# Router bookkeeping of a mixture-of-experts step on one core: float32 against bf16 operands for the counting and list products

## The reference

```python
g_logits = (x @ rgw + rgb).astype(jnp.float32)
g_sel = jnp.argmax(g_logits, axis=-1)
e_logits = (x @ rew + reb).astype(jnp.float32).reshape(-1, N_GROUPS, EXPERTS_PER_GROUP)
e_sel = jnp.take_along_axis(e_logits, g_sel[:, None, None], axis=1)[:, 0]
top_v, top_i = lax.top_k(e_sel, TOP_K_IN_GROUP)
...
for e in range(N_EXPERTS):
    h = jax.nn.silu(x @ wg[e]) * (x @ wu[e])
    y = y + gates[:, e:e + 1] * (h @ wd[e]).astype(jnp.float32)
```

## Time and profile before

| what | value |
|---|---|
| median of 3 runs | 1059.52 us (1059.48, 1059.52, 1064.51) |
| profiled execution | 1065.51 us, of which 1063.3 us is the span |
| PE busy | 935.1 us, 88% of the span |
| DVE, ACT, POOL busy | 380.2, 238.3, 81.6 us |
| mean granted TensorE clock | 0.936 |
| memory traffic | 208.76 MB, 196 GB/s on average |

### The profile page before, as it was taken

The page is one execution under the profiler, slowest core; times in us unless marked ns, Lnnn a source line. Parts: engine busy times, 40 slices in busy tenths (PEclk is TensorE's granted clock), DMA queues, the critical chain, the costliest instruction groups (busy, mean ns, idle before and its releaser), DMA issues.

```text
span 1063.3 us, 15679 instructions
## 1 busy us (share of the span) xinstructions
PE 935.1 (88%) x6393; PEld 495.7 (47%) x6393; DVE 380.2 (36%) x806; ACT 238.3 (22%) x600; POOL 81.6 (8%) x96
## 2 busy tenths in 40 slices
PE   3996999999999999978978997899998978892996
PEld 3453556654547676665435554443333423341442
DVE  3205645562325747354542125221111111112345
ACT  3116212220123223353212112110000000001335
POOL 1000000000004533000000000100000000002100
PEclk9999999997999989978688999899999989997998
DMA  6454233033246662164603606379999999995101
GB/s 208 178 218 178 31 139 139 4 137 142 79 167 221 235 192 82 42 216 139 198 10 114 259 22 256 127 275 347 378 394 401 402 396 388 407 405 208 41 22 61
DMA packets 72099, 208.76 MB, mean 196 GB/s; under 512 B 15937, under 2 KB 48148, under 8 KB 67548
## 3 DMA queue, kind: packets, MB, share of 16 engines
q1 hardware_dynamic: 57344, 184.73, 46.9%
q0 software_dynamic: 3936, 14.22, 4.0%
q10 hardware_dynamic: 10748, 8.80, 2.6%
HBM read 188.31 MB, written 38.25 MB: 213 GB/s over the span
## 4 chain that ended last, share of the span: by engine, by line
PE 71%; DMA 11%; DVE 10%; ACT 4%; issue 2%; SPq 1%; ACTq 0%; POOL 0%; DVEq 0%; POOLq 0%
PE ps L1930 17%; DMA EXPERT<-in_moe_w_up 9%; PE ps L2354 8%; PE ps L1935 8%; PE ps L2240 6%; PE ps L2460 6%; PE ps L2389 3%; PE ps L2363 3%; PE ps L1965 2%; PE ps L2309 2%; PE ps L2011 1%; PE ps L2092 1%; PE ps L2038 1%; PE ps L1939 1%; PE ps L1914 1%
## 5 line engine op out<-in xcount | busy, mean ns | idle before, releaser
L1930 PE MATMUL ps<-xT,EXPERT 128*128 128x512 f32 x384 | 182.1, 619 | 1.2 <-DVE EXPERT L1263 1.2
L2354 PE MATMUL ps<-EXPERT,aF 128*32 128x512 f32 x1024 | 117.3, 611 | 20.5 <-DMA EXPERT<-in_moe_w_up 12.2
L1935 PE MATMUL ps<-EXPERT,xT 128*128 128x384 f32 (+1 forms) x384 | 121.7, 459 | 1.6 <-ACT EXPERT L917 1.6
L1930 PEld LDWEIGHTS ps<-xT,EXPERT 128*128 128x128 f32 x384 | 71.4, 196 | 79.5 <-issue 75.8
L1935 PEld LDWEIGHTS ps<-EXPERT,xT 128*128 128x128 f32 x384 | 78.8, 238 | 24.6 <-issue 3.5
L2354 PEld LDWEIGHTS ps<-EXPERT,aF 128*32 128x32 f32 x1024 | 34.3, 112 | 99.4 <-issue 81.2
L2460 PE MATMUL ps<-EXPERT 128*128 128x512 f32 x128 | 58.7, 618 | 5.3 <-DVE EXPERT L1891 5.3
L2389 PE MATMUL ps<-EXPERT,dF 128*32 128x512 f32 x512 | 58.2, 595 | 3.3 <-ACT dF L1168 3.3
L2240 PE MATMUL ps<-EXPERT,xT 128*128 128x512 f32 x128 | 60.0, 621 | 1.1 <-ACT xT L1087 1.1
L1843 DVE TENSOR_TENSOR dF<-dF,ps 64x512 f32<-64x512 f32 x16 | 11.0, 690 | 138.6 <-ACT dF L1164 138.6
L1164 ACT ACTIVATE dF<-ps 64x512 f32<-64x512 f32 x16 | 9.4, 590 | 207.4 <-PE ps L2354 207.4
(11 more groups left out here) (439 smaller groups left out, 1234.8 us busy)
## 6 DMA issues: line engine op xcount, KB each, us to landing
EXPERT<-in_moe_w_gate SPq DMA_DIRECT2D x16, 2048.0 KB, 15.9
EXPERT<-in_moe_w_up SPq DMA_DIRECT2D x16, 2048.0 KB, 20.9
EXPERT<-in_moe_w_down SPq DMA_DIRECT2D x16, 2048.0 KB, 21.8
EXPERT<-in_w_in SPq DMA_DIRECT2D x13, 1536.0 KB, 6.6
out_win_sample<-in_cache_win SPq DMA_DIRECT2D x16, 1022.0 KB
aF<-in_cache_k_diff SPq DMA_DIRECT2D x32, 192.0 KB, 2.5
aF<-in_cache_v_diff SPq DMA_DIRECT2D x32, 192.0 KB, 2.5
Yd<-wk ACTq DMA_DIRECT2D x34, 128.0 KB, 9.0
```

The source lines that it names most:

```text
L1930: last = t.matmul(ps[:, u % 2, :], W_[:, c, c0:c0 + w], xT[:, c, 0:SEQ], start=(c == 0), stop=(c == DC - 1))
L1935: last = t.matmul(ps[:, u % 2, 0:w], rows_, W_[:, c, c0:c0 + w], start=(c == 0), stop=(c == DC - 1))
L2354: last = t.matmul(ps[32 * q:32 * q + 32, 2, :], xgT[:, c, 32 * (q % 2):32 * (q % 2) + 32], w[:, c, :], start=(c == 0), stop=(c == DC - 1))
```

## The change

C, the ones, tri, Rsel and Tsel become bf16. Zeros, ones and counts of at most two are exact in bf16; a token number up to 519 is not. So the number is split in two exact parts, the low seven bits and the rest (a multiple of 128), and Tsel has twice as many columns of data: for each block 33 with the low part and 33 with the high part. The sums stay float32 in PSUM. The list step thus has 20 products in place of ten. POOL sets a bf16 table of ones; DVE makes the parts once, ahead of the first residual addition.

```diff
+        parts = take(2 * T5, 2)
-        C = take(T5, NE)
+        C = take(T5 * NE // 2, dt=BF16).rearrange("p (i e) -> p i e", i=T5)
-        Tsel = take(2 * T5, MAXT)
+        hot = take(T5 * MAXT, dt=BF16).rearrange("p (m j) -> p m j", m=2 * T5)
+        Tsel = take(2 * T5 * MAXT, dt=BF16).rearrange("p (m a j) -> p m a j", m=2 * T5, a=2)
-        Rsel = dF_[:, 0:2 * T5 * P].rearrange("p (m n) -> p m n", m=2 * T5)
+        Rsel = dF_[:, 0:T5 * P].bitcast(BF16).rearrange("p (m n) -> p m n", m=2 * T5)
...
             seq(g.memset(tri, 1.0))
+            seq(g.memset(onesb, 1.0))
...
             seq(v.tensor_tensor(tokf, tokf, valid, ALU.mult))
+            seq(v.tensor_copy(iti[:, 0:T5], tokf))
+            seq(v.tensor_scalar(iti[:, T5:2 * T5], iti[:, 0:T5], P - 1, None, ALU.bitwise_and))
+            seq(v.tensor_tensor(iti[:, 0:T5], iti[:, 0:T5], iti[:, T5:2 * T5], ALU.subtract))
+            for k in range(2):
+                v.tensor_copy(parts[:, k * T5:(k + 1) * T5, 0], iti[:, T5:2 * T5])
+                seq(v.tensor_copy(parts[:, k * T5:(k + 1) * T5, 1], iti[:, 0:T5]))
...
-            seq(v.tensor_tensor(Tsel, iotaf[:, 0:MAXT].unsqueeze(1).to_broadcast([P, 2 * T5, MAXT]), f2(tk, MAXT), ALU.is_equal))
-            v.tensor_tensor(Tsel.rearrange("p (k i) j -> p k i j", k=2), Tsel.rearrange("p (k i) j -> p k i j", k=2),
-                            tokf.unsqueeze(1).unsqueeze(3).to_broadcast([P, 2, T5, MAXT]), ALU.mult).then_inc(S_["rank_ok"], 1)
+            seq(v.tensor_tensor(hot, iotaf[:, 0:MAXT].unsqueeze(1).to_broadcast([P, 2 * T5, MAXT]), f2(tk, MAXT), ALU.is_equal))
+            v.tensor_tensor(Tsel, hot.unsqueeze(2).to_broadcast([P, 2 * T5, 2, MAXT]), f3(parts, MAXT),
+                            ALU.mult).then_inc(S_["rank_ok"], 1)
...
-                t.matmul(ps[:, 1, k * NE:T5 * NE], ones[:], Cf[:, 0:(T5 - k) * NE], start=False, stop=(k == T5 - 1))
+                t.matmul(ps[:, 1, k * NE:T5 * NE], onesb, Cf[:, 0:(T5 - k) * NE], start=False, stop=(k == T5 - 1))
...
-                last = t.matmul(ps[:, 1, 96:96 + MAXT], Rsel[:, m], Tsel[:, m], start=(m == 0), stop=(m == 2 * T5 - 1))
+                for k in range(2):
+                    last = t.matmul(ps[:, 1, 96:96 + MAXT], Rsel[:, m], Tsel[:, m, k], start=(m + k == 0),
+                                    stop=(m + k == 2 * T5))
```

More of the change, by code:

```diff
@@ L472, in hybrid_kernel @@
         toki = take(T5, dt=I32)
-        tri = take(P)
+        tri = take(P // 2, dt=BF16)
+        onesb = take(P // 2, dt=BF16)
+        parts = take(2 * T5, 2)
         before = take(4, 4)
@@ L575, in f2, with f3 @@
             return ap.unsqueeze(2).to_broadcast([ap.shape[0], ap.shape[1], n])
+        def f3(ap, n):
+            return ap.unsqueeze(3).to_broadcast([ap.shape[0], ap.shape[1], ap.shape[2], n])
         def rows_of(buf, i):
@@ L2320, in _ @@
             for k in range(1, T5):
-                t.matmul(ps[:, 1, k * NE:T5 * NE], ones[:], Cf[:, 0:(T5 - k) * NE], start=False, stop=(k == T5 - 1))
+                t.matmul(ps[:, 1, k * NE:T5 * NE], onesb, Cf[:, 0:(T5 - k) * NE], start=False, stop=(k == T5 - 1))
             for k in range(T5):
-                last = t.matmul(ps[:, 1, T5 * NE:(T5 + 1) * NE], ones[:], C[:, k], start=(k == 0), stop=(k == T5 - 1))
+                last = t.matmul(ps[:, 1, T5 * NE:(T5 + 1) * NE], onesb, C[:, k], start=(k == 0), stop=(k == T5 - 1))
             last.then_inc(S_["rank_pe"], 1)
```

## The result

Over 14 runs each, the changed kernel has a median of 1053.07 us, the kernel before 1059.51 us: 6.4 us less. The ratio is 0.9926, with an interval from 0.9899 to 0.9953, so the gain is clear of noise and lies between 0.47% and 1.01%, which is 5.0 to 10.7 us. The ratio leaves aside runs far above their kernel's fastest, so it is not the quotient of the medians (0.9939). The predicted 1055.0 us was 1.9 us too high, inside the range; but "faster by over 0.5%", which came, had a chance of only 0.30 against 0.66 for "within".

The account below looks back on a forecast made before the run. The router stage, a line of waits ahead of the first expert, was taken as the bound. Terms of -1.8 + 0.34 - 3.1 = -4.55 us off the median 1059.52 gave 1055.0 us, range 1052.0 to 1060.0.

Parts of the forecast that it names:

- What bounds the stage: From output projection to first expert: a line of waits; a microsecond off the router stage is one off the end.
- rows(0) moves less than 3 us: Sign that the prediction is wrong; rows(0), ahead of the first expert, was expected near 679.8 us, from 684.32.
- Rank step: Ten float32 products on PE, 2.15 us, become ten bf16 passes of 0.35 us: gain 1.8 us (1.45 to 1.95).
- Selection tables: On DVE, ahead of the list products: the multiply grows by 330 elements, a loss of 0.34 us.
- Rival D: DVE writes bf16 at half pace in the selection tables: 2.7 us lost, 1057.3 us; chance 0.05.
- List step: List products on PE: 20 float32 passes of 4.29 us become 20 bf16 passes of 1.2; gain 3.1 us (1.5 to 3.9).
- Rivals B and C: PE weight loads: B, a set 0.107 us each, 1056.6 us, chance 0.09; C, loads cannot overlap, 1058.3 us, chance 0.05.
- The work behind: pproducts(2), behind the list products, starts 4.5 us sooner and keeps its length: cost nothing (1.1 us gained to 1.5 lost).
- Rival A: The clock rises sooner, 3 us after pproducts(2) starts: 1.1 us more gain, 1053.9 us; chance 0.20.
- Hidden work: Seven small DVE instructions, 1.3 us, covered by the residual addition's 2.52 us wait for W_out; POOL's ones also hidden.
- Rival E: The clock stays at 1.2 GHz through pproducts(2) to (4): 8.1 us more, 1063.1 us; chance 0.04.
- Rival F: A load or gather independent of this stage holds the first expert: no gain, 1059.5 us; chance 0.04.

Follow-up runs that it names:

- the filler's row: The changed kernel with seven unread float32 products (14 passes) on PE while it waits for the selection tables; ratio 0.9934 against the kernel before.
- the bf16 list alone: The changed kernel with tri, ones and C back in float32, so only Rsel, Tsel and the list products are bf16; ratio 0.9971 against the kernel before.
- the rank experiment: The kernel before with only tri, ones and C in bf16; ratio 0.9964 against the kernel before.
- 60 float32 passes: The kernel before with its float32 list products done three times over; one execution, each further pass cost 0.213 us.
- two blocks moved: The changed kernel with pproducts(2) and pproducts(3) ahead of the list products on PE; ratio 0.9892 against the kernel before.
- one block moved: The changed kernel with pproducts(2) ahead of the list products on PE; ratio 0.9907 against the kernel before.

## Why the prediction was right and wrong

- *What bounds the stage.* Right. What came off the router stage came off the way to rows(0), and the weight stream followed rows(0) by the same 12.88 us where no dip came between. The sign "rows(0) moves less than 3 us" I should have set from a start: in absolute position rows(0) moved only 0.77 us, because this execution was already 5.94 us late at W_out; from the first rank pass it moved 6.20.
- *Rank step.* Predicted gain 1.8 us, measured 1.88. DVE's wait fell to 0.53 us; I had written 0.8.
- *Selection tables.* Predicted loss 0.34, measured 0.35. Rival D, a slow write of bf16, is out: 1.49 and 0.50 us stayed.
- *List step.* **This term was mis-sized.** I gave 20 passes 1.2 us, the trace 0.59: a gain of 3.7 and not 3.1. The failed step is "at half clock the load is some 0.03 us and 33 columns are 0.0275: 0.06 us each". I had split the 0.07 us of the one bf16 pair into columns and a load and doubled the load. No load shows at all: 0.0285 us is close to the columns' time at half clock (0.0275), and at full clock a pass takes (0.67 - 0.18)/19 = 0.026 us by the filler's row, its single pass being 0.18, and that is twice its 0.014 us of columns. So at full clock something other than the columns sets some 0.026 us, and the pass is almost blind to the clock. What that is was not tried.
- *Rivals B and C* fail at the same place. The rule in the Trainium skill, "TensorE: Matmul & The Clock Gate", section LDWEIGHTS, would have made 20 loads 2.1 us, as an estimate; they and their matmuls take 0.59. The section on weight-path modes of the same page of the Trainium skill, by which a full bf16 load of 128 columns is quicker, fits that spacing. A single load is still recorded at 0.103 to 0.115 us at half clock, where rival C had 0.196; but 20 of them pass in 0.59 us, so each begins long before the one ahead has ended, which is what C denied.
- *The work behind.* **This term was set at nothing, and the traces differ by 0.95 us**: "I leave that length as it is: cost nothing". pproducts(2) took 5.28 and 5.31 us, before 6.23. Rival A had the clock rise sooner, at 1.1 us and a chance of 0.20, and in size it came. Its reason, the short list step, is not borne out: behind the bf16 list alone the block took 6.03 us, behind the unchanged float32 list of the rank experiment 5.88, behind 60 float32 passes 5.35. The rise lay 2.4 to 5.2 us behind the start of the block in the various traces and meets a given kernel differently. The kernel before has one trace, so how much of the 0.95 belongs to the change stays open.
- *Hidden work.* Right: POOL and the small DVE instructions cost nothing, the residual addition still waits 1.81 us.
- *The sum.* -1.88 + 0.35 - 3.70 - 0.95 = -6.2 us, R to the last tenth, and the medians differ by 6.4; so near a match is partly luck, since the ratio's interval is 5.0 to 10.7 us. The passes and the multiply alone make 5.2 us of it. My -4.55 lay below the 0.5% bound of 5.3 us by 0.75, and the two errors, 0.6 and 0.95, both went one way: the first alone would not have crossed the bound. With a spread of several microseconds over so near a bound, 0.66 for "within" was too firm.
- *Rival E*, the clock staying down, did not happen behind the list, but its kin did: a dip at the first expert in five of 13 traces, worth 14.58 - 12.88 = 1.7 us in the changed kernel. I had named no such thing.
- *Rival F* is refuted by rows(0), which came sooner from the first rank pass and waited for no transfer. With two blocks moved it does wait for the gather, but that is no case of F: the gather hangs on the list, so on this stage.

## What to carry to other kernels

In this kernel a float32 product of 128 weight columns and few moving ones cost the same whatever it moved, two passes of 0.11 us at full clock and 0.21 at half, and a bf16 one under 0.03 us: integers split into exact bf16 parts are worth twice as many products. But look first at what the clock does where they stand and at what work could fill the wait ahead of them; here, moving four products into the gap gained as much as the change of type, and, by R, halved what that change was still worth. Where the runs scatter more than the gain, compare a stretch between two fixed instructions across traces, and take more than one trace of each kernel before a difference of a microsecond is put down to the change: the clock alone can make it.

## What the hardware showed that I had not expected

- A bf16 product with 128 weight columns and 33 moving ones follows the one before after 0.0285 us at half clock and 0.026 at full; the float32 one, as two passes, 2 x 0.214 and 2 x 0.112.
- 12.8 us of float32 passes back to back, PE busy throughout, did not lift the granted clock from 0.50. In the version with one block moved the clock fell at about 662.9, 1.4 us after PE had taken up work again behind a gap of 1.87 us.
- At half clock, pairs of 64 and 64 weight columns pass in 0.054 us, pairs of 96 and 32 in 0.33 us.
- The granted clock can fall at the first expert in some executions of a kernel and not in others of the same one: the changed kernel's first gate and up products took 8.77 us in one trace and 7.07 in the other.
